# A weight ring of eight slots that becomes four, with seven slots of key and value weights kept for both token tiles

## What is computed

```python
for l in range(2):
    mkv = (mem @ w_mem_kv[l])...
    if l == 0:
        ...                                   # gated linear attention
    else:
        h = x @ b_w_in[0]                     # queries (2304) and memory queries (256)
        mix = _dilated_attention(qd, shared_k, shared_v)
    mo = _mem_attn(qm, mkv[:, :, 0], mkv[:, :, 1])
    y = concatenate([mix, mo]) @ w_out[l]
    x = _layer_norm(ALPHA * x + y, ...)
    f = _peer(x, peer_w_q[l], peer_sub_keys[l], peer_u[l], peer_v[l])
    x = _layer_norm(ALPHA * x + f, ...)
    if l == 0:
        kv = x @ shared_w_kv                  # shared_k (768) and shared_v (768) for layer 1

def _peer(...):                               # per token: 8 heads x 16 experts
    h = einsum('td,thkd->thk', x, u[expert])
    out = einsum('thk,thkd->td', gelu(h) * gate, v[expert])
```

## Time and profile before

| what | value |
|---|---|
| median of 3 runs | 2075.84 us (2075.06 to 2077.94) |
| the profiled execution | 2079.32 us, its span 2077.5 us |
| PE busy | 1889.9 us (91% of the span) |
| DVE busy | 1385.7 us (67%) |
| ACT busy | 892.3 us (43%) |
| POOL busy | 599.4 us (29%) |
| moved by DMA | 712.93 MB, mean 343 GB/s |
| gathers (software queue) | 550.86 MB |
| weight loads and other direct transfers of the main hardware queue | 159.39 MB |
| mean granted clock of TensorE | 0.981 |

### The profile page before, as it was taken

One profiled execution on the slowest core, in us unless ns is written; L12 is line 12 of the kernel. 1 busy time (PEld: TensorE's weight loads), 2 busy tenths in 40 slices (PEclk: granted clock), 3 DMA queues, 4 the chain that ended last, 5 costly groups with the idle time before them and its releaser, 6 DMA issues. The chain is left out here.

```text
span 2077.5 us, 24540 instructions
## 1 busy us (share of the span) xinstructions
PE 1889.9 (91%) x7948; PEld 1177.2 (57%) x7948; DVE 1385.7 (67%) x2957; ACT 892.3 (43%) x2409; POOL 599.4 (29%) x563
## 2 busy tenths in 40 slices
PE   8999999999998989877999998879999989878776
PEld 8888678887954645432565534546665455332222
DVE  8778566666738776899534645767855566994444
ACT  5657454454633343334324623333455334343332
POOL 0002200000003444343433334333335433444331
PEclk9999999999999999999999999999999999999999
DMA  6633555544549999999999999999999999999997
GB/s 244 224 130 111 192 193 184 194 170 168 217 153 383 421 421 402 421 416 421 405 421 421 421 421 421 421 421 404 421 420 412 422 421 409 421 413 421 422 421 303
DMA packets 99915, 712.93 MB, mean 343 GB/s; under 512 B 11088, under 2 KB 11216, under 8 KB 14800
## 3 DMA queue, kind: packets, MB, share of 16 engines
q0 software_dynamic: 77040, 550.86, 64.4%
q1 hardware_dynamic: 22320, 159.39, 20.2%
q10 hardware_dynamic: 432, 1.16, 0.1%
HBM read 710.32 MB, written 1.05 MB: 342 GB/s over the span
## 5 line engine op out<-in xcount | busy, mean ns | idle before, releaser
L1436 PE MATMUL bank<-arena 128*128 128x512 f32 x2048 | 977.6, 615 | 163.7 <-ACT arena L2054 162.9
L2492 DVE SCALAR_TENSOR_TENSOR arena<-arena,x_tok 128x1024 f32<-128x1024 f32 x512 | 619.1, 1225 | 456.1 <-DMA arena<-peer_uv,arena 452.4
L2211 POOL DMA_INDIRECT arena<-peer_uv,arena x512 | 566.2, 1106 | 892.5 <-PE bank L1436 738.4
L1436 PEld LDWEIGHTS bank<-arena 128*128 128x128 f32 x2048 | 374.4, 194 | 650.6 <-issue 336.3
L2047 ACT ACTIVATE arena<-arena 128x1 f32<-128x1 f32 x512 | 103.1, 201 | 852.7 <-DVE arena L2492 852.1
L905 PEld LDWEIGHTS bank<-xT,weight_ring 128*128 128x128 f32 x1408 | 186.5, 193 | 39.0 <-issue 32.0
L2041 ACT ACTIVATE arena<-const_tile,arena 128x128 f32<-128x128 f32 x512 | 198.2, 387 | 0.0
L2054 ACT ACTIVATE arena<-arena 128x128 f32<-128x128 f32 x512 | 197.7, 386 | 0.5
L905 PE MATMUL bank<-xT,weight_ring 128*128 128x128 f32 (+1 forms) x1408 | 196.4, 293 | 0.8 <-DVE xT L2235 0.8
L905 PE MATMUL bank<-x_low_high,z_high 128*128 128x512 f32 (+1 forms) x480 | 136.5, 352 | 0.0
L1181 PE MATMUL bank<-x_split,w_split 128*128 128x512 f32 x704 | 128.7, 341 | 2.6 <-DVE x_split L2772 2.6
(11 more groups left out here) (319 smaller groups left out, 1966.9 us busy)
## 6 DMA issues: line engine op xcount, KB each, us to landing
weight_ring<-weights SPq DMA_DIRECT2D x150, 1024.0 KB, 4.9
arena<-peer_uv,arena POOLq DMA_INDIRECT x512, 14.5
row_ring<-rows_in POOLq DMA_DIRECT2D x10, 512.0 KB, 4.9
arena<-weights POOLq DMA_DIRECT2D x5, 512.0 KB, 8.5
const_tile<-consts POOLq DMA_DIRECT2D x1, 1849.0 KB, 9.2
kept_keys<-weights POOLq DMA_DIRECT2D x3, 512.0 KB, 8.7
x_tok<-x_in SPq DMA_DIRECT2D x2, 512.0 KB, 4.4
memT<-memT_in POOLq DMA_DIRECT2D x1, 1024.0 KB, 6.1
```

The source lines that it names most:

```text
L1436: ins = pe.matmul(b[:, :], diag[n % DIAGS], gbuf[n % GBUF][:, 1, h * 512:(h + 1) * 512], start=n % P == 0, stop=n % P == P - 1)
L2211: pool.indirect_dma_start(gbuf[n % GBUF].rearrange("p a d -> p (a d)"), None, peer_uv, bass.IndirectOffsetOnAxis(ap=expert[t][:, s:s + 1]. ...
L2492: dve.scalar_tensor_tensor(u, u, 1.0, x[:, t, :], ALU.mult, ALU.mult, accum_out=hdot[:, s:s + 1])\
```

## The change

From layer 1's weights on, the ring has four slots (two pairs) in place of eight. The stream is cut at slot 200, the last multiple of eight ahead of layer 1 (slots 200 and 201 are the last memory values). The upper four ring slots then hold four more kept slots: together with the three of the old place, now `kept_own`, that makes seven, the six slots of keys and the first of values, used by both tiles. SP loads these four with four transfers of 512 KB each once PE has given back the ring slots 4 to 7 for the last time; the three others are still loaded by POOL. A layer-1 tile takes 45 slots from the ring in place of 49. SP's loop covers the stream up to slot 200, and the loads after it are written out one by one. The block of keys on PE waits, once per tile, for both groups of kept loads. Nothing of the arithmetic changes.

```diff
-KEPT_KEYS = 3
+KEPT = 7
+KEPT_OWN = 3
+NARROW = 4
...
+    narrow_from = len(out) // RING * RING
...
-    layer = keys[KEPT_KEYS:] + list(v.transpose(0, 2, 1, 3).reshape(6, P, SLOT))
+    layer = keys + list(v.transpose(0, 2, 1, 3).reshape(6, P, SLOT))
     layer += slots_of_columns(q)
     layer += slots_of_rows(a["w_out_2"][1])[:NK - 2] + slots_of_columns(a["peer_w_q_2"][1])
+    layer, kept = layer[KEPT:], layer[:KEPT]
     out += layer * NT
...
+        kept = [kept_own[:, i, :] for i in range(KEPT_OWN)]
+        kept += [ring[:, i, :] for i in range(NARROW, RING)]
...
+        def place_of(n):
+            return n % RING if n < narrow_from else (n - narrow_from) % NARROW
+        def loads_of(n):
+            return n // RING + 1 if n < narrow_from else narrow_from // RING + (n - narrow_from) // NARROW + 1
...
-                pe.wait_ge(sem(f"weights_loaded{n % RING // PAIR}"), 16 * (n // RING + 1))
+                pe.wait_ge(sem(f"weights_loaded{place_of(n) // PAIR}"), 16 * loads_of(n))
...
+            def layer_weights(i):
+                return kept[i] if i < KEPT else next_weights()
...
                     if part % 4 == 0:
-                        wt["values"] = next_weights()
+                        wt["values"] = layer_weights(DSLOTS + part // 4)
...
-                            pe.wait_ge(sem("kept_keys_loaded"), 16 * KEPT_KEYS)
-                        kept = kept_keys[:, i, :] if i < KEPT_KEYS else None
-                        block_of((f"dil_k_{o}_{i // 4}", 0), i % 4, 4 if i < 4 else 2, tile_xT, kept=kept)
+                            pe.wait_ge(sem("kept_loaded_early"), 16 * KEPT_OWN)
+                            pe.wait_ge(sem("kept_loaded_late"), 16 * (RING - NARROW))
+                        block_of((f"dil_k_{o}_{i // 4}", 0), i % 4, 4 if i < 4 else 2, tile_xT, w=layer_weights(i))
...
-            for n in range(pairs // per * per, pairs):
-                s = n % per
-                sp.wait_ge(sem("weight_free"), PAIR * (n + 1))
+            for m in range(-(-(wt["n"] - narrow_from) // PAIR)):
+                if m == narrow:
+                    for i in range(NARROW, RING):
+                        sp.wait_ge(sem("weight_free"), narrow_from + i + 1)
+                        sp.dma_start(kept[KEPT - RING + i], kept_source(KEPT - RING + i)).then_inc(sem("kept_loaded_late"), 16)
+                s, n = m % narrow, narrow_from // PAIR + m
+                sp.wait_ge(sem("weight_free"), PAIR * (n + 1) + (RING - NARROW if m >= narrow else 0))
```

More of the change, by code:

```diff
@@ L533, in weight_slots @@
     keys = slots_of_columns(kv[:, :768])
-    layer = keys[KEPT_KEYS:] + list(v.transpose(0, 2, 1, 3).reshape(6, P, SLOT))
+    layer = keys + list(v.transpose(0, 2, 1, 3).reshape(6, P, SLOT))
     layer += slots_of_columns(q)
     layer += slots_of_rows(a["w_out_2"][1])[:NK - 2] + slots_of_columns(a["peer_w_q_2"][1])
+    layer, kept = layer[KEPT:], layer[:KEPT]
     out += layer * NT
     out += [np.zeros((P, SLOT), np.float32)] * (len(out) % PAIR)
-    out += keys[:KEPT_KEYS] + [np.zeros((P, SLOT), np.float32)] * (KEPT_KEYS % PAIR)
+    out += kept + [np.zeros((P, SLOT), np.float32)] * (KEPT % PAIR)
     out += peer_q[:4] + slots_of_columns(bw[:, 2304:]) + slots_of_rows(a["w_out_2"][1])[NK - 2:]
@@ L544, in weight_slots @@
     w = w.reshape(-1, PAIR, P, SLOT).transpose(0, 2, 1, 3).reshape(-1, P, PAIR * SLOT)
-    return w, z_slot, ffn_slot, part_slots
+    return w, z_slot, ffn_slot, part_slots, narrow_from
 def constant_columns(a):
@@ L632, in build @@
         rows = sb("row_ring", [P, NROW, D])
-        kept_keys = sb("kept_keys", [P, KEPT_KEYS, SLOT])
+        kept_own = sb("kept_own", [P, KEPT_OWN, SLOT])
         cst = sb("const_tile", [P, n_const])
@@ L689, in area, with kept_source @@
             return v
+        kept = [kept_own[:, i, :] for i in range(KEPT_OWN)]
+        kept += [ring[:, i, :] for i in range(NARROW, RING)]
+        assert len(kept) == KEPT
+        def kept_source(i):
+            return weights[n_slots - 4 - (KEPT + 1) // 2 + i // PAIR, :, i % PAIR * SLOT:(i % PAIR + 1) * SLOT]
         ident = c("ident")
@@ L876, in build @@
         wt = {"n": 0, "owed": 0}
+        narrow_from = where["narrow_from"]
+        assert narrow_from % RING == 0
+        def place_of(n):
+            return n % RING if n < narrow_from else (n - narrow_from) % NARROW
+        def loads_of(n):
+            return n // RING + 1 if n < narrow_from else narrow_from // RING + (n - narrow_from) // NARROW + 1
         @block.tensor
@@ L887, in next_weights @@
                 wt["n"] = n + 1
-                return ring[:, n % RING, :]
+                return ring[:, place_of(n), :]
             def held_weights(i):
@@ L1450, in add_slot, with block_of @@
                     pe.sem_inc(sem("psum_filled"), 2)
-            def block_of(key, i, n, lhs, tokens=P, kept=None):
+            def layer_weights(i):
+                return kept[i] if i < KEPT else next_weights()
+            def block_of(key, i, n, lhs, tokens=P, w=None):
                 b = begin(key) if i == 0 else bank(key)
-                w = next_weights() if kept is None else kept
+                w = next_weights() if w is None else w
                 for k in range(NK):
@@ L1636, in _ @@
                 sp.dma_start(x[:, t, :], x_in[t * P:(t + 1) * P, :]).then_inc(sem(f"x_loaded{t}"), 16)
-            pairs, per = -(-wt["n"] // PAIR), RING // PAIR
-            with sp.Fori(0, pairs // per) as i:
+            per, narrow = RING // PAIR, NARROW // PAIR
+            with sp.Fori(0, narrow_from // RING) as i:
                 for s in range(per):
@@ L2170, in _ @@
                 load_row(pool, n)
-            for i in range(KEPT_KEYS):
-                pool.dma_start(kept_keys[:, i, :], weights[n_slots - 6 + i // 2, :, i % 2 * SLOT:(i % 2 + 1) * SLOT])\
-                    .then_inc(sem("kept_keys_loaded"), 16)
+            for i in range(KEPT_OWN):
+                pool.dma_start(kept[i], kept_source(i)).then_inc(sem("kept_loaded_early"), 16)
             pool.wait_ge(sem("psum_filled"), ids[("att_turn", 2 * len(UNITS) - 1)] + 1)
@@ L3015, in prepare @@
         at += v.shape[1]
-    weights, where["z_slot"], where["ffn_slot"], where["part_slots"] = weight_slots(a)
+    weights, where["z_slot"], where["ffn_slot"], where["part_slots"], where["narrow_from"] = weight_slots(a)
     arrays = {
```

## The result

The changed kernel takes 2085.26 us (median of 8 runs, 2080.48 to 2092.45) against 2075.49 us before: ratio 1.0049, 95% interval 1.0039 to 1.0058, so 8 to 12 us slower. The forecast was +5, with a range from -5 to +12.

A forecast was written before the change was run, and what follows sets the result against it. DMA bytes at 421 GB/s were taken as the bound. PE at 1628 us: 2.0 + 7.0 + 3.4 - 2.5 - 1.5 = +8.4; less cushion 8.1, plus loads 5.0: +5.3 us, forecast 2081.0 us, range -5 (2071) to +12 (2088).

The forecast's parts named there:

- Bytes, -5.0: Whole weight stream: 148 loads' worth in place of 150, at 2.49 us each, saves 5.0 us at the DMA bound.
- Number and place of the waits: Layer 1, 1040 to 1680 us: some 15 PE waits for ring weights, 2 to 4 us long at the output products.
- The output's two waits, 3.4 each: Tile 1's output product: two successive pairs land late, so PE waits 3.4 us for each, 7 us together.
- The wait of the queries and values in tile 1, 2.0 us: Layer 1, tile 1: three short query waits and one in the values, 2 us together, bounds 0 and 7.
- T: Time for a ring load to land: 9.2 us median beside gathers, taken as 8.0 for tile 1's queries and values.
- The lead from tile 0, -1.5: Tile 0: DMA is 5.0 us ahead by postponed loads, waits cost 3.5 of it, so 1.5 us reaches tile 1.
- Clock, +3.4: Tile 1's output product: two falls of PE's clock to 1.2 GHz behind the waits, 1.7 us each, bounds 0 and 7.
- The sum at tile 1's end: PE at 1628 us, after tile 1's output product: waits, clock, old wait and lead together make it 8.4 us late.
- The cushion and the loads still to come, -8.1 and +5.0: After 1628 us: slack between gather issue and use gives back 8.1 us; seven loads left in place of five add 5.0.
- Rival 1, all hidden: Layer 1's ring: loads land in about 7 us, waits are hidden and only saved bytes count: -5 us, 2070.9; chance 0.20.
- Rival 2, a draw: Tile 1: waits as forecast but the clock holds, PE 5.0 us late, cushion 9.6: +0.4, 2076; chance 0.20.
- Rival 3: Tile 1's output product and queries: T = 9.2 throughout, clock falls after most waits: +13.3, about 2088; chance 0.15.

The follow-up runs named there:

- alone: Seven slots kept but the ring left at eight slots, against the kernel before (four kept slots hold wrong weights, same work): ratio 0.9983.
- early return: The changed kernel, but each ring slot is given back when its own products are done, not by the next slot's first product: 0.9980 against the kernel before.
- single slots for tile 0 only: The changed kernel with ring slots loaded one by one for tile 0, still in pairs for tile 1: 1.0037 against the kernel before.
- output rows spread: The changed kernel with the output product's rows reordered so that each pair load has three steps to land, not two: 1.0033 against the kernel before.
- single slots: The changed kernel with the four ring slots loaded one by one, 512 KB each, in place of pairs: 0.9992 against the kernel before.
- single slots for tile 1: The changed kernel with pair loads kept in tile 0 and ring slots loaded one by one in tile 1: 1.0014 against the kernel before.

## Why the prediction was right, and where its terms were off

The sign, the mechanism and the place were as forecast; the size was half of what came (+5.3 against +10.2), within the range. Several terms were off, some of them against each other.

- *Bytes, -5.0.* Right within the scatter: -3.5 (-5.4 to -1.7) alone, and -4.2 with early return.
- *Number and place of the waits.* Forecast some 15; 14 came, eight in tile 0 (20.1 us), five in tile 1's stretch (11.1) and one in its PEER queries (2.6).
- *The output's two waits, 3.4 each.* They were 3.39 and 1.35. The first was exact by luck: its load was wanted 6.0 us after it was issued, not 5.7, and took 9.4, not 9.1. The second was shorter by the 1.8 us that the clock fall between them added to PE's products. The forecast put down both the full wait and the fall.
- *The wait of the queries and values in tile 1, 2.0 us.* This is the step that failed most. I took T = 8.0 since DMA would be emptier. The three waits of the queries were 2.12, 2.47 and 1.78 us, 6.4 in all, with 8.9, 10.6 and 9.9 us from the issue to PE's start; the one in the values did not come. That is near the 7 of my upper end, T = 9.2. The traces of two variants tell landing times too: with single slots for tile 0 only, the pairs of tile 1 landed after 5.0 to 11.0 us, median 9.3, and with the output rows spread all pairs after 6.6 to 11.1 us, median 9.1. Why it is not shorter with fewer loads in front was not tried.
- *The lead from tile 0, -1.5.* It was +1.2. Without its waits tile 0's stretch gains the 5.0 us (391.4 to some 386); with them it loses 6.2 to 6.7 again, where I took 3.5 and an upper end of 5.0.
- *Clock, +3.4.* The size came, the place did not. I had both falls behind the output's waits. One came there (1615 us) and lengthened its products by 2.39 + 2.85 - 2 x 1.72 = 1.8 us, all of it time in which PE would have waited. The other came behind a wait of the queries, at 1461 us, where the forecast had none: 3.06 + 2.58 - 2.05 - 1.88 = 1.7 us. A longer wait at 1500 us had none behind it:

```profile
1460.98 3.06 PE L927 MATMUL bank<-xT,weight_ring 128*128 128x128 f32 x16 [2.12 <-DMA weight_ring<-weights]
1463.83 2.58 PE L1458 MATMUL bank<-arena 128*128 128x512 f32 x4
...
1500.63 2.05 PE L927 MATMUL bank<-xT,weight_ring 128*128 128x128 f32 x16 [2.47 <-DMA weight_ring<-weights]
```

- *The sum at tile 1's end.* 11.1 (waits) + 3.5 (clock) - 2.5 (the old wait) = 12.1 of the 12.7 us by which that stretch grew. With the lead that makes +14.0, where +8.4 was forecast.
- *The cushion and the loads still to come, -8.1 and +5.0.* -3.1 forecast, -3.8 came. Both parts can be read from the table of stretches. In the last column the change has seven loads to come, as forecast, the kernel before five, the early return six, and single slots 13 halves, 6.5. The loads: single slots, with 1.5 more than before (3.7 us), take 4.2 to 4.5 us longer there; the early return, with one more (2.5 us), only 0.5. The cushion, once the loads are taken out at 2.49 us each: 3.8 + 5.0 = 8.8 us against the kernel before, 8.0 + 1.2 = 9.2 against single slots for tile 1, 4.3 + 2.5 = 6.8 against the early return. In the changed kernel a gather issued at 1643.59 starts its dot at 1651.94, 8.35 us and no longer 14.5: the cushion is used up, as foreseen, to about the 7.8 of the fastest gather.

```profile
1643.59 1.74 POOL L2240 DMA_INDIRECT arena<-peer_uv,arena  x1 [0.30 <-PE bank L1458]
...
1651.94 1.23 DVE L2521 SCALAR_TENSOR_TENSOR arena<-arena,x_tok 128x1024 f32<-128x1024 f32 x1 [1.28 <-DMA arena<-peer_uv,arena]
```

- *Rival 1, all hidden,* fell with every wait that came, and its landing time of 7 us did not come either (medians 9.1 and 9.3). Its end, some 5 us faster than before, is what the early return makes of the kernel. *Rival 2, a draw,* had the clock holding, which it did not, and PE 5.0 us late at the end of tile 1's stretch, where it was 14.0; its cushion of 9.6 was nearer. *Rival 3* had the right T for the queries and went too far with the clock; its sum is +13.3, about 2089 us, and not the 2088 that it gives.

## What to carry to other kernels

A ring's depth is worth what its hand-over makes of it: ask how many steps lie between the moment a slot is given back and the moment the refill is wanted, and set that against the landing time beside the other traffic, not the landing time alone. Before a fall of the clock is added to a wait, ask whether the next wait takes it in. Where a consumer returns a slot by its first work on the next one, return it instead by the next instruction that it runs anyway; here that turned +0.5% into -0.2% with nothing else changed. And where two resources are both at their limit, as PE and DMA here, bytes taken from one did not pay for waits added to the other in series.

## What was not expected

The total idle time of PE barely changed, yet the kernel lost 10 us: 33.7 us of waits for weights took the place of 36 us of waits for diagonals. Only 11.1 us of them stand in tile 1's stretch, where PE had no time to spare and DMA moved less (399 GB/s), but with the one wait of 2.6 us behind it they cost the most: 7 to 9 us by the medians, against 2.5 to 4.6 for the 20.1 us in tile 0. And the length of a wait does not tell whether the clock falls behind it: in tile 1's queries it fell after 2.12 us and not after 2.47, and with the output rows spread it did not fall after 3.07.
